# Down projections of the first block in seven products, and layer 0's modulation tiles loaded by GpSimd and multiplied in its linear stages

## The reference, cut to what matters

```python
def conv_ffn(xn, w_up, conv_w, conv_b, w_down):
    h = causal_depthwise_conv(xn @ w_up, conv_w) + conv_b
    g, u = jnp.split(h, 2, axis=-1)
    return (jax.nn.gelu(g) * u) @ w_down
...
    proj = xn @ w_in                        # fox_diff_mixer, first block, layer 0
    fq, fk, fv, ff, dq, dk, dv = jnp.split(proj, cuts, axis=-1)
    log_f = jax.nn.log_sigmoid((ff + fox_bf).astype(jnp.float32)).transpose(0, 2, 1)
```

```python
    mod = (silu_c @ lp["w_mod"] + lp["b_mod"])[:, None, :]
    sh1, sc1, gt1, sh2, sc2, gt2 = jnp.split(mod, 6, axis=-1)
    ...
    modc = (silu_cc @ lp["w_mod"][:, :n_mod_c] + lp["b_mod"][:n_mod_c])[None, None, :]
```

## Time and profile before

| | us |
|---|---|
| Times of three runs: lowest, median, highest | 2518.7, 2523.35, 2523.64 |
| The profiled execution, its own time | 2517.16 |
| Its span, first to last instruction | 2515.1 |
| TensorE busy | 2475.1 |
| VectorE busy | 1270.1 |
| GpSimd busy | 550.1 |
| ScalarE busy | 544.5 |
| Mean rate of the DMA engines | 133 GB/s |

### The profile page before, as it was taken

One profiled execution on the slowest core, in us unless ns is written; L12 is line 12 of the kernel. 1 busy time (PEld: TensorE's weight loads), 2 busy tenths in 40 slices (PEclk: granted clock), 3 DMA queues, 4 the chain that ended last, 5 costly groups with the idle time before them and its releaser, 6 DMA issues.

```text
span 2515.1 us, 36716 instructions
## 1 busy us (share of the span) xinstructions
PE 2475.1 (98%) x14000; PEld 2020.7 (80%) x14000; DVE 1270.1 (51%) x2602; ACT 544.5 (22%) x1198; POOL 550.1 (22%) x474
## 2 busy tenths in 40 slices
PE   9989999999999999999999999999999999999999
PEld 6857899986799998745567666888888875999999
DVE  3034178751325887324846763544542247435774
ACT  1131122111212220213630001222200215212220
POOL 1000135200212540001002321323241010232543
PEclk9999999999999999999999999999999999999999
DMA  6323265643334566121023662121222120243453
GB/s 236 134 101 117 84 226 186 261 180 134 117 134 168 193 226 234 67 81 39 1 84 142 222 252 104 67 100 67 113 92 80 67 94 26 104 167 150 167 193 109
DMA packets 40018, 334.59 MB, mean 133 GB/s; under 512 B 3920, under 2 KB 10192, under 8 KB 22736
## 3 DMA queue, kind: packets, MB, share of 16 engines
q1 hardware_dynamic: 39888, 332.78, 35.7%
HBM read 331.72 MB, written 1.05 MB: 132 GB/s over the span
## 4 chain that ended last, share of the span: by engine, by line
PE 92%; DVE 3%; DMA 3%; POOL 1%; ACT 1%; issue 1%; SPq 0%; DVEq 0%; POOLq 0%; ACTq 0%
PE PS L769 25%; PE PS L569 21%; PE PS L2763 6%; PE PS L1029 6%; PE PS L1529 6%; PE PS L1719 4%; PE PS L2804 4%; PE PS L1338 3%; PE PS L1704 3%; PE PS L2282 2%; PE PS L1349 2%; PE PS L1361 2%; DMA slot<-in_weights 2%; PE PS L436 1%; PE PS L750 1%; PE PS L2420 1%
## 5 line engine op out<-in xcount | busy, mean ns | idle before, releaser
L569 PE MATMUL PS<-XN,slot 128*128 128x256 f32 (+1 forms) x1184 | 296.8, 411 | 0.8 <-DVE XN L508 0.8
L769 PE MATMUL PS<-SQ,slot 128*128 128x128 f32 (+1 forms) x1984 | 294.5, 301 | 2.2 <-DVE slot L865 2.2
L569 PEld LDWEIGHTS PS<-XN,slot 128*128 128x128 f32 x1184 | 224.5, 190 | 69.9 <-issue 42.5
L769 PEld LDWEIGHTS PS<-SQ,slot 128*128 128x128 f32 x1984 | 268.1, 191 | 15.5 <-DVE slot L865 2.6
L769 PE MATMUL PS<-XN,slot 128*128 128x128 f32 (+1 forms) x1664 | 250.0, 301 | 0.0
L569 PE MATMUL PS<-arena,slot 128*128 128x256 f32 x1088 | 236.6, 379 | 0.8 <-DMA slot<-in_weights 0.7
L769 PEld LDWEIGHTS PS<-XN,slot 128*128 128x128 f32 x1664 | 226.1, 192 | 10.7
L569 PEld LDWEIGHTS PS<-arena,slot 128*128 128x128 f32 x1088 | 206.3, 190 | 30.8 <-issue 1.9
L892 DVE SCALAR_TENSOR_TENSOR arena<-PS,small,arena 128x255 f32<-128x255 f32 (+2 forms) x352 | 174.9, 544 | 47.3 <-ACT arena L836 47.1
L836 ACT ACTIVATE arena<-PS,small 128x256 f32<-128x256 f32 (+1 forms) x176 | 105.1, 616 | 376.3 <-DVE PS L925 237.6
L480 POOL TENSOR_TENSOR SQ<-SQ 128x512 f32<-128x512 f32 (+1 forms) x36 | 42.3, 1178 | 536.6 <-ACT SQ L446 536.1
(11 more groups left out here) (291 smaller groups left out, 3661.8 us busy)
## 6 DMA issues: line engine op xcount, KB each, us to landing
slot<-in_weights SPq DMA_DIRECT2D x85, 2048.0 KB, 7.8
arena<-in_mod SPq DMA_DIRECT2D x96, 512.0 KB, 3.4
slot<-in_weights SPq DMA_DIRECT2D x16, 2816.0 KB, 9.7
slot<-in_weights SPq DMA_DIRECT2D x24, 1536.0 KB, 6.7
slot<-in_weights SPq DMA_DIRECT2D x5, 1024.0 KB, 4.8
slot<-in_weights SPq DMA_DIRECT2D x2, 2176.0 KB, 8.8
arena<-in_c SPq DMA_DIRECT2D x3, 1024.0 KB, 10.9
small<-in_small SPq DMA_DIRECT2D x1, 1982.0 KB, 17.2
```

The lines of the kernel that those rows point to most:

```text
L569: mm = pe.matmul(o, l, r, start=k == 0, stop=k == len(terms) - 1, skip_group_check=True)
L769: mm = pe.matmul(PS[:, bank, 0:h], lhs[:, k * P:(k + 1) * P], rhs(k), start=first and k == 0, stop=last and k == 3, skip_group_check=True)
```

## The change

It has two parts.

The first block's two down projections take the form with seven products that the second block's have. `vector_down_seven` learns to add without a gate, and in a1 the context's norm stands behind the second pair (`then`) on TensorE and VectorE.

The 48 modulation tiles are no longer loaded by SyncE in a0 and a1. GpSimd issues all of them in layer 0 (`gpsimd_mod_loads`), into three slots, each load behind the use of the tile three before. VectorE multiplies tiles 0 to 7 ahead of the gate chain, 8 to 15 ahead of the copy of `foxin`'s job 2, 16 to 22 ahead of job 6's, 23 to 32 behind job 7's, 33 to 39 between the reads of `mixout0`, and 40 to 47 between those of `xo0`. The conditioning vectors come through SyncE behind the third slab, and again in `mixout0`; their Silu stands on ScalarE behind the exponentials of lambda.

```diff
+        MOD_SLOTS, MOD_OUT, MOD_XO = 3, 35, 40
+        MODC = [X[:, :, T:2 * T].rearrange("p (g j) t -> p g j t", g=2), area(12288, 2, 4, T)]
+        mod_slots = [[area(at, 4, T) for at in (16384, 17408, third)] for third in (12288, 14592)]
...
+        def vector_mod_tiles(dve, *tiles):
+            for n in tiles:
+                w = mod_slots[n >= MOD_OUT][n % MOD_SLOTS]
+                c = MODC[n >= MOD_XO]
+                if n in (0, MOD_XO):
+                    dve.wait_ge(*of("silu_c", int(n >= MOD_XO)))
+                dve.wait_ge(sems[f"mod_landed{n % MOD_SLOTS}"], 16 * (n // MOD_SLOTS + 1))
+                for g in range(2):
+                    if g == 0 and n:
+                        dve.wait_ge(*of("mod_tile", n - 1, 0))
+                    vector_mod_product(dve, w, c[:, g, :, :], MOD[:, 0, n, g:g + 1], w if g else MODP)\
+                        .then_inc(*tick(VD, "mod_tile", n, g))
+                if n % MOD_HALF == MOD_HALF - 1:
+                    vector_mod_end(dve, 0, n // MOD_HALF, [("mod_tile", n, 1)])
+
+        def gpsimd_mod_loads(pool, tiles):
+            for n in tiles:
+                if n == 2:
+                    pool.wait_ge(*of("memkv0", "job", 3))
+                if n == MOD_OUT:
+                    pool.wait_ge(*of("subln", "out", 3, 0))
+                if n >= MOD_SLOTS:
+                    pool.wait_ge(*of("mod_tile", n - MOD_SLOTS, 1))
+                pool.dma_start(mod_slots[n >= MOD_OUT][n % MOD_SLOTS], mod_in[n].rearrange("p (j t) -> p j t", t=T))\
+                    .then_inc(sems[f"mod_landed{n % MOD_SLOTS}"], 16)
+
+        def scalar_silu_c(act, f):
+            act.wait_ge(sems["loaded_c"], 16 * (f + 1))
+            act.activation(MODC[f], MODC[f], ACT.Silu).then_inc(*tick(SD, "silu_c", f))
...
-        def tensor_down_seven(pe, s, pairs, n):
+        def tensor_down_seven(pe, s, pairs, n, then=None):
...
+                if then and p == 1:
+                    then(pe)
...
+                if gate is None:
+                    return dve.tensor_tensor(x, src, x, ALU.add)
...
+                add(scalar=lambda a: scalar_silu_c(a, 0), vector=lambda d: vector_mod_tiles(d, *range(0, 8)),
+                    gpsimd=lambda p: gpsimd_mod_loads(p, range(0, MOD_OUT)))
...
+                def vector_foxin(dve, jobs=fox_jobs):
+                    for j, job in enumerate(jobs):
+                        vector_mod_tiles(dve, *{2: range(8, 16), 6: range(16, 23)}.get(j, ()))
+                        reads_linear(dve, VD, "vector", "foxin", [job], j)
+                    vector_mod_tiles(dve, *range(23, 33))
...
+                add(scalar=lambda a: scalar_silu_c(a, 1), gpsimd=lambda p: gpsimd_mod_loads(p, range(MOD_OUT, 43)))
...
+                        [(33, 34), (35, 36, 37), (38, 39), ()])
...
+                add(gpsimd=lambda p: gpsimd_mod_loads(p, range(43, MOD_TILES)))
...
+                        [(40, 41, 42), (43, 44, 45), (46, 47), ()])
```

More of the change, by code:

```diff
@@ L605, in conv_spec @@
             return n, taps, centre
[L608 to L616, removed]
+        MOD_HALF = MOD_TILES // 2
+        MOD_SLOTS, MOD_OUT, MOD_XO = 3, 35, 40
         def vector_mod_product(dve, w, c, total, scratch):
@@ L1610, in add_ffn @@
             n = T * len(segs)
-            early = block == "b"
             add(tensor=lambda pe: tensor_up_seven(pe, s, norm, segs), scalar=lambda a: scalar_up_seven(a, s, segs),
                 vector=lambda d: vector_up_seven(d, s, norm, segs),
-                gpsimd=lambda p: gpsimd_up_seven(p, s, n, (lambda e: gpsimd_down_sums(e, s, 0)) if early else None))
-            if block == "a":
-                add(vector=lambda d: [vector_mod_tile(d, s, r, g) for r in range(5, 11) for g in range(2)])
+                gpsimd=lambda p: gpsimd_up_seven(p, s, n, lambda e: gpsimd_down_sums(e, s, 0)))
+            tensor_then = vector_then = None
             if aside:
@@ L1627, in add_ffn @@
                 return
-            if block == "b":
-                add(tensor=lambda pe: tensor_down_seven(pe, s, DK // 2, n),
-                    vector=lambda d: vector_down_seven(d, s, DK // 2, n, gate),
-                    gpsimd=lambda p: gpsimd_down_seven(p, s, DK // 2, n))
-                return
-            add_out(f"d{s}", lambda k: H[:, k, 0:T * len(segs)], None, FM, segs, gate,
-                    then=(lambda pe: tensor_norm(pe, aside_s, aside_units)) if aside else None,
-                    needs=lambda k: (s, "h", k) if k >= FM - 2 else (s, "h", PAIRS - 1, "last"),
-                mod=s if block == "a" else None)
@@ new lines, in add_ffn, with add_out @@
+            add(tensor=lambda pe: tensor_down_seven(pe, s, DK // 2, n, tensor_then),
+                vector=lambda d: vector_down_seven(d, s, DK // 2, n, gate, vector_then),
+                gpsimd=lambda p: gpsimd_down_seven(p, s, DK // 2, n))
+        def add_out(s, rhs, ready, k_tiles, segs, mod):
+            def reads(j, bank):
+                return [("vector", lambda e: e.tensor_tensor(
+                    X[:, 2 * j:2 * j + 2, 0:T], PS[:, bank, :].rearrange("p (i t) -> p i t", i=2),
+                    X[:, 2 * j:2 * j + 2, 0:T], ALU.add))]
+            jobs = feature_jobs(rhs, ready, DK, reads, k_tiles=k_tiles, segs=segs)
@@ L2232, in two_blocks @@
                 if l == 1 else None)
-            prev_ready = after_out(f"da{l}", [0], None)
+            prev_ready = [[(f"da{l}", "read", 2 * p, 1)] for p in range(DK // 2)]
         add_norm("final", norm_x("final", X, X, lambda m, g: col("final_norm", m), prev_ready, [0]))
@@ L3040, in _ @@
                             load(g0 + j, n // P // P, src[turn * 2 + j])
-                            if s[0] == "a" and j == 0:
-                                sp.wait_ge(*of(s, "mod_product", 1, turn=turn, back=1))
-                                load_mod(int(s[1]), 0, turn)
                     g = g0 + 2 * W_TURNS
-                    if s[0] == "a":
-                        for rs in ((7,), (), (8,), range(9, 15), range(15, 18), range(18, MOD_HALF)):
-                            sp.wait_ge(*slot_free(g))
-                            load(g, len(table[g][1]), piece(g))
-                            g += 1
-                            for r in rs:
-                                sp.wait_ge(*(of(s, "mod_product", 1, turn=W_TURNS - 1) if r == 7 else
-                                             of(s, "mod_tile", r - 4, 1)))
-                                load_mod(int(s[1]), r)
                     continue
```

114 lines of the change are left out of this document (26 added, 88 removed).

## The result

The changed kernel takes 2530.52 us (median of 7 runs, 2528.48 to 2536.4) against 2521.55 for the one before (7 runs, 2517.88 to 2523.64). The ratio is 1.0037, 95% interval [1.0028, 1.0046]: slower, by about 9 us. I had forecast 2517 us and faster; the rival "slab first" had said 2526.2 to 2532.4. The profiled execution took 2528.48 us, with a span of 2526.7 against 2515.1: 11.6 us more.

A forecast was written before the change was run, and what follows sets the result against it. TensorE was taken as the bound, busy 2475.1 of 2515.1 us. Gain -11.0 plus cost 6.0 gave -5.0: 2512.2 us from the profiled 2517.16, 2518.3 from the median; 2517 us was named, range 2509 to 2533.

The forecast's parts named there:

- slab first: Rival: layer 0 tiles issued while a slab is in flight wait for it; cost 20.0 us, net +9.0; chance 0.33.
- The transfers: Step on layer 0's tile loads beside 2 MB slabs: 5.0 us on TensorE instead of 2.1.
- Cost 6.0 us: Layer 0's forecast loss: 5.0 us before job 6 of the input projection, 1 us at the attention.
- even-sharing sum: Input projection: tile and slab queues share bandwidth evenly, job 2's copy at 115.8 against 110.9, 5.0 us wait; chance 0.40.
- slack of 3.5 us: Layer 0: VectorE done at about 154.8, against an attention that needs it at 156.24 + 2.1.
- Gain 11.0 us: Both down projections save 10.4 us, the start of layer 1's up projection 0.3, the end of its down projection 0.3.
- The check on the context norm: Layer 1's down projection: the norm's VectorE work ends before the third pair's fifth product needs its operand, 1 us to spare.
- gain not reached: Rival: the seven-product down projections meet new waits, giving 7 us instead of 11, net -1; chance 0.12, mixtures near zero included.
- The order's floor of 2.1 us: Input projection of layer 0: TensorE waits 2.1 us before job 6 through VectorE's new order, with no transfer late.
- Software issue 1 us: Layer 0: GpSimd's issue, 0 to 1 us a tile beyond SyncE's, takes the slack and costs 1 us at the attention.
- GpSimd hidden: After the first output projection: GpSimd's standing at its loads delays nothing, as the last tiles are used before its next norm.
- faster by more: Whole kernel faster by more than 0.2%, 5 us; chance given as 0.36.

The follow-up runs named there:

- the three edits together: Kernel after with GpSimd's context-norm sums later, tiles 0 to 7 before lambda, and four load slots instead of three; 2508.38 us, ratio 0.9944 to the kernel before.
- four slots: Kernel after with four slots instead of three for tiles 0 to 32, nothing else moved; one execution, span 2514.1 us.
- without tiles: Kernel after without the 48 modulation loads and their products, only the bias kept; 2509.55 us, ratio 0.9959 to the kernel before.
- half tiles: Kernel after with half the bytes of each modulation tile loaded (256 KB), same number of loads; one execution, span 2529.3 us.
- tiles earlier: Kernel after with the Silu of c and tiles 0 to 7 moved before lambda; 2512.28 us, ratio 0.9969 to the kernel before.

## Why the prediction was wrong, point by point

**The step that failed** is the choice in "The transfers": "I take the middle, both queues sharing evenly." I had one row near the question, a tile right behind a slab at about 10 us, and set it aside because it was on one queue. Between bounds of 3.4 and 10 us I chose the middle, and for that choice there was no row. The packets by queue in the kernel after show what came in its place, first from 100.60 to 103.00, then from 103.00 to 105.50, with a tile issued at 99.40 and a slab at 98.02 (columns as above):

```profile
q1 hardware_dynamic: 62, 1.02, 103.2%
...
q1 hardware_dynamic: 50, 0.82, 76.5%
q0 software_dynamic: 54, 0.22, 22.1%
```

For 3.6 us after its issue the tile has no packet. After that both queues move one packet in turn, 54 against 50, and as the slab's are four times as large, the tile gets a fifth of the bytes and not half. Both together hold it to the slab's end. The issues of the kernel after, worked out from its list issue by issue:

| Tile issued at | slab nearest, issued at | tile's time to landing | slab's time to landing |
|---|---|---|---|
| 81.41 | none near | 3.4 | |
| 97.11 | 98.02, so 0.9 later | 3.6 | 8.5 |
| 99.40 | 98.02 | 7.8 | 8.5 |
| 101.69 | 98.02 | 6.8 | 8.5 |
| 112.23 | 111.83 | 9.7 | 9.9 |
| 148.14 | 146.54 | 10.0 | 11.0 |

A tile issued behind a slab lands 0.7 us or less after the slab (0.2 with half the bytes); the next ones follow at about 1.3 us each. Those issued 0.5 us and more ahead of it took 3.6 to 4.1 us, one issued 0.4 ahead 6.4. With 4.6 us of cover each slab stalls VectorE. The timeline of the kernel after at the first two slabs:

```profile
99.40 0.53 POOL L637 DMA_DIRECT2D arena<-in_mod  x1 [1.76 <-DVE modulation L612]
...
107.27 1.22 DVE L612 CUSTOM_DVE_ANT_1 arena<-arena,X 128x1024 f32<-128x1024 f32 x1 [3.58 <-DMA arena<-in_mod]
...
112.23 0.53 POOL L637 DMA_DIRECT2D arena<-in_mod  x1 [1.76 <-DVE modulation L612]
...
121.95 1.23 DVE L612 CUSTOM_DVE_ANT_1 arena<-arena,X 128x1024 f32<-128x1024 f32 x1 [4.23 <-DMA arena<-in_mod]
```

**Cost 6.0 us** measured 20.0. Before job 6 the even-sharing sum had 5.0 and got 5.38, but for another reason: tile 7 was issued 0.5 us ahead of its slab and came in time, and tile 12 alone was held, 3.58 us. The failure shows behind that: VectorE's slack of 3.5 us before the attention was to be touched by "a little", and waits of 4.23, 0.85, 2.11, 5.75 and 4.10 us came. All but the 0.85 are for a tile issued beside a slab. That one is for a tile issued at 124.63, with no slab about, which took 5.1 us; why, no run shows. The rival slab first had 20.0 in all, with 12.0 for the attention's side (10.64 plus 2.0 of clock) and 8 before job 6 (5.38 plus 1.6 of clock). Its mechanism is right; that its total is exact is partly luck, since it held tile 7, put a wait of 2 us before job 4 that did not come, and knew nothing of the clock.

**Gain 11.0 us** is 8.9 in the trace (5.25 + 2.6 + 0.6 + 0.4). In its parts: a0's down -5.2, measured -5.25; a1's -5.2, measured -2.6; the start and the end of layer 1's -0.3 each, measured -0.6 (over the whole stretch between the two calls) and -0.4. The check on the context norm was made on VectorE alone ("hidden, with 1 us to spare", and the third pair indeed has no wait). I did not look at GpSimd's list, where the norm's sums now stand beside the operand sums of the first pair. Of the rival "gain not reached" this is the size, 2.7 us of the 4 it had.

**The order's floor of 2.1 us**: 1.72, right. **Software issue 1 us**: wrong, there is none to see; most tiles with no slab about land in 3.4 to 3.9 us, against SyncE's 3.4. The Trainium skill warns of a lock that keeps GpSimd from writing descriptors (SBUF — State Buffer, section on SBUF's two separate sides); it shows in none of these, issued while VectorE multiplied. **GpSimd hidden**: right; its sums of the norm after `mixout0` begin only at 253.24, behind the last loads, but TensorE's products there stand 20.5 us later than before like all around them.

**What the chances missed.** Slab first had 0.33 against 0.40, and the number given was that of even sharing. (The chance of "faster by more" adds up to 0.35, half of 0.40 and 0.15, not to 0.36.) The asymmetry was in the text: 13 tiles in 40 us with 4.6 us of cover, and any landing over 7 us decides against the change.

What stays open: why the tile's first packet comes so late behind a slab. It is not the tile's bytes (halving them made it land no earlier), not the software issue, and not the size of the slab's packets (3.7 us after the issue with 16 KB, 4.0 with 4 KB). Whether it is the queue, or simply that the slab was issued first, no run here tells; the tile was never issued from another queue.

## What to carry to other kernels

A transfer's time must be read beside the traffic that it will meet: count the cover (slots x time per tile) against the landing time behind the largest transfer, not against its median alone. If nothing in the trace shows it, the nearest row decides, and depth or an earlier start is cheap insurance: one slot more took 12.6 us off here, between two single executions, and the three edits together 22 us between the medians. When a part is moved, look at every engine's list for what it now stands beside, also at those that do nothing for the critical path.

## What the hardware showed unexpectedly

- Behind waits of 3.19, 5.38 and 10.64 us TensorE went on at a mean granted clock of 0.50 to 0.65 in windows of 2.5 to 4 us (kernel after and four slots), and jobs 6 and 7 took 15.4 to 15.8 us instead of 13.84; behind 1.72 us they took 13.9. These waits cost 1.6 to 2 us more than their length. Short waits differ between traces: behind those of 1.2 and 2.0 us in layer 1's down projection the clock was 1.00 in the kernel after, and 0.50 for some microseconds without tiles, with half tiles and with tiles earlier. Behind the norm before the first up projection it was 0.50 in the kernel before (330.0 to 333.3) as in the one after (349.0 to 352.3).
- A 512 KB tile behind a 2 MB slab took 7.8 to 10.0 us and its half 8.4, against 3.5 alone. The slab took 8.3 to 11.0 instead of 7.7. The tile's first packet starts 3.0 to 4.1 us after its issue instead of 1.2 to 1.5, and then the two queues take turns packet by packet.
- VectorE and GpSimd adding float32 in SBUF at once slow each other: 2.68 against 1.61 us, and 2.6 against 1.35.
